# Residual rows of both routers turned back by TensorE, and the sparse attention's head in three rounded passes

## What is computed

```
for i in range(2):
    m = short_conv_mixer(x, ...) if i == 0 else dsa_mixer(x, ...)
    x = layer_norm(ALPHA * x + m, ln1_g[i], ln1_b[i])
    f = hier_moe(x, ...)        # router, then 64 experts of width 256, two for each token
    x = layer_norm(ALPHA * x + f, ln2_g[i], ln2_b[i])
```

## Time and profile before

| what | value |
|---|---|
| median of 3 runs | 2770.97 us (2769.46 to 2772.14) |
| the profiled execution | 2773.85 us, of which the span is 2772.0 us |
| busy share: PE, DVE, ACT, POOL | 90%, 49%, 29%, 4% |
| chain that ended last: PE, DMA, DVE | 64%, 23%, 7% |

### The profile page before, as it was taken

The page is one execution under the profiler, slowest core; times in us unless marked ns, Lnnn a source line. Parts: engine busy times, 40 slices in busy tenths (PEclk is TensorE's granted clock), DMA queues, the critical chain, the costliest instruction groups (busy, mean ns, idle before and its releaser), DMA issues.

```text
span 2772.0 us, 37468 instructions
## 1 busy us (share of the span) xinstructions
PE 2491.0 (90%) x14707; PEld 1794.8 (65%) x14708; DVE 1363.5 (49%) x2406; ACT 817.0 (29%) x1400; POOL 98.6 (4%) x80
## 2 busy tenths in 40 slices
PE   6999999999999999999888888878999978888887
PEld 4888788787678888787644444445765854444443
DVE  4555645633442225544654444434956474444444
ACT  3222333246232224322212112122367322121121
POOL 0000002000000000000020000003000030000000
PEclk9999999999999999999999999999999989999999
DMA  7655432401233332223389999984230449999976
GB/s 263 199 184 188 166 99 72 137 31 61 107 106 99 99 98 87 88 92 122 137 350 422 422 422 422 422 339 162 67 107 1 152 190 379 422 422 422 422 308 283
DMA packets 200620, 593.78 MB, mean 214 GB/s; under 512 B 9473, under 2 KB 125393, under 8 KB 151121
## 3 DMA queue, kind: packets, MB, share of 16 engines
q1 hardware_dynamic: 196736, 575.47, 54.0%
q0 software_dynamic: 3504, 16.63, 1.9%
...
HBM read 590.32 MB, written 7.41 MB: 216 GB/s over the span
## 4 chain that ended last, share of the span: by engine, by line
PE 64%; DMA 23%; DVE 7%; issue 3%; ACT 2%; SPq 1%; DVEq 0%; ACTq 0%
PE bank L1988 39%; DMA arena<-in_exp_w 17%; PE bank L2344 6%; PE bank L2078 5%; DMA ring<-in_exp_w 3%; PE bank L2364 2%; PE bank L2571 1%; SPq L579 1%; PE bank L2249 1%; PE bank L2468 1%; PE bank L2538 1%; PE bank L2168 1%; DVE ring_low L1207 1%; PE bank L2313 1%; PE bank L2371 1%
## 5 line engine op out<-in xcount | busy, mean ns | idle before, releaser
L1988 PE MATMUL bank<-parts 128*128 128x512 f32 x2624 | 817.8, 393 | 13.5 <-DVE parts L1446 5.5
L1988 PEld LDWEIGHTS bank<-parts 128*128 128x128 f32 x2624 | 493.5, 189 | 116.0 <-issue 7.5
L1988 PE MATMUL bank<-parts,ring_low 128*128 128x512 f32 x1312 | 513.7, 392 | 0.0
L1207 DVE TENSOR_TENSOR ring_low<-ring,parts 128x2048 fp32r<-128x2048 f32 x106 | 238.2, 2251 | 219.2 <-ACT parts L769 219.0
L2344 PE MATMUL bank<-ring,arena 128*32 128x256 f32 x2112 | 276.9, 417 | 54.2 <-DMA arena<-in_exp_w 54.2
L2344 PE MATMUL bank<-arena 128*32 128x256 f32 x2112 | 277.2, 417 | 28.9 <-issue 25.2
L769 ACT ACTIVATE parts<-ring 128x2048 fp32r<-128x2048 f32 x106 | 198.9, 1877 | 282.4 <-DMA ring<-in_w_ffn_in 123.1
L1988 PEld LDWEIGHTS bank<-parts,ring_low 128*128 128x128 f32 x1312 | 247.9, 189 | 52.1
L2371 PE MATMUL bank<-parts 128*128 128x512 f32 x496 | 169.2, 447 | 43.8 <-DVE parts L1731 23.0
L2344 PEld LDWEIGHTS bank<-ring,arena 128*32 128x32 f32 x2112 | 133.9, 115 | 110.5 <-issue 77.6
L1988 PE MATMUL bank<-ring_low 128*128 128x512 f32 x576 | 195.1, 397 | 1.7 <-ACT arena L1008 1.7
...
## 6 DMA issues: line engine op xcount, KB each, us to landing
arena<-in_exp_w SPq DMA_DIRECT2D x192, 1024.0 KB, 17.7
ring<-in_exp_w SPq DMA_DIRECT2D x192, 1024.0 KB, 19.5
...
```

Of the source, the lines that this page charges most:

```text
L1207: TTn(ring_low[:, n, 0:nk * cols], ring[:, n, 0:nk * cols], buf.bitcast(F32), ALU.subtract)\
L1988: i = mm(o, a[:, cols[0], cols[1]], b, start=first_ and n == 0, stop=last_ and n == 2)
```

## The change

1. **Residual, both routers.** POOL's eight instructions on `HT` and its loads of two rows are gone. PE turns `U` (which holds the same activation with gain and bias in it) back tile by tile into PSUM, 32 transposes of 128 x 128, between the router's steps, and ACT copies the 4 tiles of 128 x 1024 into `HT`. PE waits for the first copy ahead of the last tile, for two of them ahead of the first `gather` and for all ahead of the first turn. POOL's loads for the last norm come after it, with a wait in the last norm.
2. **Plan.** DVE's `rows_high` is moved ahead of two of the plan's steps (L1704, L1705).
3. **Head.** `c_kv`, `k_idx` and `w_idx` become one product of 200 columns in the tail (full float32), loaded as two pieces into one slot. `q_idx` is made in three passes. ACT rounds `U` by token tile in the norm (`rounded_rows`), DVE takes the rests so too (`row_rests`), the two index tiles of weights are rounded into `WHQ`. The loads of `stream_b` change slots and all of its first four wait for the last turn's `up` alone, not for its `down`.
4. **POOL's other eight instructions** (L731, L736) wait for the choice of keys (`mask`), where they ran beside the head.

```diff
-for n, c in enumerate((8, 9, 10)):
-    stream_b.append((tall(A["attn_w_in"], 256 * c, 256 if c < 10 else 200), KT, 256 if c < 10 else 200,
-                     ("qi_mm", "qi_mm", "kv_mm")[n], (1, 3, 2)[n]))
+latent_index = [(tall(A["attn_w_in"], HEADS2 * LATENT, LATENT), 0, LATENT),
+                (tall(A["attn_w_in"], HEADS2 * LATENT + LATENT + IDX_HEADS * IDX_DIM, 72), LATENT, LATENT + 72)]
+stream_b.append((latent_index, KT, LATENT + 72, "kv_mm", TT))
+for n in range(2):
+    stream_b.append((tall(A["attn_w_in"], (HEADS2 + 1) * LATENT + 256 * n, 256), KT, 256, "qi_mm", 2 * n + 2))
...
             for n in range(len(stream_b)):
-                if n < 5:
-
-                    sp.wait_ge(sem("turn_y" if n < 2 else "turn_ab"), last * 2 + 2)
+                if n < 4:
+
+                    sp.wait_ge(sem("turn_ab"), last * 2 + 2)
                 else:
...
-        pool.wait_ge(sem("moe_logits"), 4 * layer + 4)
-        for v, row in enumerate((layer, 2 + layer) + ((5, 7) if layer else ())):
-            pool.dma_start(ROWS[:, v], lnrows[row].partition_broadcast(P)).then_inc(sem("ln_vectors"), 16)
-        pool.wait_ge(sem("xt_low"), 4 * layer + 4)
-        pool.wait_ge(sem("moe_plan"), layer + 1)
-        pool.wait_ge(sem("ln_vectors"), 160 if layer else 64)
-        for t in range(TT):
-            st.did(pool.tensor_tensor(HT[:, t], HT[:, t], ROWS[:, 0], ALU.mult))
-        for t in range(TT):
-            if t == 0:
-                st.wait()
-            pool.tensor_tensor(HT[:, t], HT[:, t], ROWS[:, 1], ALU.add).then_inc(sem("resid"), 1)
-        if layer == 0:
+        if layer:
+            pool.wait_ge(sem("resid_tp"), 8)
+            for v, row in ((2, 5), (3, 7)):
+                pool.dma_start(ROWS[:, v], lnrows[row].partition_broadcast(P)).then_inc(sem("ln_vectors"), 16)
+        else:
...
-            pool.wait_ge(sem("ln_vectors"), 80)
+            pool.wait_ge(sem("ln_vectors"), 48)
             pool.wait_ge(sem("lt"), 16)
+            pool.wait_ge(sem("mask"), 5)
             for t in range(TT):
...
             pool.dma_start(ROW2, lnrows[6].partition_broadcast(P)).then_inc(sem("ln_vectors"), 16)
-            pool.wait_ge(sem("ln_vectors"), 96)
+            pool.wait_ge(sem("ln_vectors"), 64)
             for t in range(TT):
...
+    def rounded_rows(t):
+        act.wait_ge(sem("u_high"), 4 + t + 1)
+        act.wait_ge(sem("u_low"), 4 + t + 1)
+        A_(UQ[0][:, :, P * t:P * t + P], U[:, :, P * t:P * t + P], ACT.Copy).then_inc(sem("t_high"), 1)
+
     def layer_norm(j):
...
                 rounded_tokens(j, t - 1)
+            if j == 1 and t >= 2:
+                rounded_rows(t - 2)
         if j < 3:
             lifted(j, 3)
+        if j == 1:
+            rounded_rows(2)
+            rounded_rows(3)
         if j in (0, 2):
...
                accum_out=RK[:, 68 + t:69 + t]).then_inc(sem("moe_ge"), 1)
+        def residual_back(t):
+
+            act.wait_ge(sem("xt_low"), 4 * l + t + 1)
+            act.wait_ge(sem("resid_tp"), 4 * l + t + 1)
+            for h in range(2):
+                x = A_(HT[:, t, 512 * h:512 * h + 512], bank[RESID_BANKS[t][h]][:], ACT.Copy)
+            x.then_inc(sem("resid"), 1)
+
+        residual_back(0)
+        residual_back(1)
         act.wait_ge(sem("moe_m"), 2 * l + 2)
         A_(RK[:, 76:80], RK[:, 72:76], ACT.Exp).then_inc(sem("moe_ge"), 1)
+        residual_back(2)
+        residual_back(3)
...
+    weights_high(split_at["dsa_qi"])
+    weights_high(split_at["dsa_qi"] + 1)
     weights_high(split_at["dsa_q"])
+    act.wait_ge(sem("var"), 1)
+    A_(DS[:, 216:224], DS[:, 192:200], ACT.Sqrt).then_inc(sem("sdev"), 1)
     for t in range(4):
...
         evac(QI[:, t], bank[t][:], "qi")
-    for k in range(KT):
-        tile_high(UQ[0][:, k], U[:, k])
-    weights_high(split_at["dsa_q"] + 1)
-    act.wait_ge(sem("var"), 1)
-    A_(DS[:, 216:224], DS[:, 192:200], ACT.Sqrt).then_inc(sem("sdev"), 1)
+        if t == 1:
+            weights_high(split_at["dsa_q"] + 1)
     def query(h):
...
         st.wait()
+        dve.wait_ge(sem("ln_vectors"), 32)
+        rows_high(i0)
         seq(TTn(past, past, turns.unsqueeze(1).broadcast_to([P, MAX_TURNS, QUADS]), ALU.mult))
         seq(nc.vector.tensor_reduce(before_it, past, AXX, ALU.add))
-        dve.wait_ge(sem("ln_vectors"), 32)
-        rows_high(i0)
         st.did(TSc(LANDS[:, of_layer], at_quad, 16.0, 16.0 + 16 * QUADS * l, ALU.mult, ALU.add))
...
+    def row_rests(t):
+        dve.wait_ge(sem("kv_mm"), t + 1)
+        dve.wait_ge(sem("t_high"), tiles_at["dsa_q"] + t + 1)
+        C = slice(P * t, P * t + P)
+        TTn(UQ[1][:, :, C], U[:, :, C], UQ[0][:, :, C].bitcast(F32), ALU.subtract).then_inc(sem("t_low"), 1)
+
+    row_rests(0)
+    row_rests(1)
+    weights_low(split_at["dsa_qi"])
     dve.wait_ge(sem("vb_mm"), 1)
...
     TSc(VB[0:HEADS2, 512:640], bank[5][0:HEADS2, 0:P], -1.0, None, ALU.mult).then_inc(sem("vb"), 1)
-
-    weights_low(split_at["dsa_q"])
-    dve.wait_ge(sem("kv_mm"), 1)
+    row_rests(2)
+    row_rests(3)
+    weights_low(split_at["dsa_qi"] + 1)
     sq = S2
     for t in range(TT):
-        src = bank[6][:, P * t:P * t + P]
-        st.did(nc.vector.tensor_copy(CKV[:, t], src))
+        at = 200 * (t % 2)
+        st.did(nc.vector.tensor_copy(CKV[:, t], bank[6 + t // 2][:, at:at + LATENT]))
     st.wait()
...
-    dve.wait_ge(sem("kv_mm"), 2)
     for t in range(TT):
-        st.did(nc.vector.tensor_copy(KI[:, t, 0:64], bank[7][:, 72 * t:72 * t + 64]))
-        st.did(TSc(W8[:, t], bank[7][:, 72 * t + 64:72 * t + 72], IDX_HEADS ** -0.5, None, ALU.mult))
+        at = 200 * (t % 2) + LATENT
+        st.did(nc.vector.tensor_copy(KI[:, t, 0:64], bank[6 + t // 2][:, at:at + 64]))
+        st.did(TSc(W8[:, t], bank[6 + t // 2][:, at + 64:at + 72], IDX_HEADS ** -0.5, None, ALU.mult))
     st.wait()
...
     nc.vector.tensor_copy(DS[:, 204:205], DS[:, 196:197]).then_inc(sem("var"), 1)
+    weights_low(split_at["dsa_q"])
     dve.wait_ge(sem("sdev"), 1)
...
     def moe(l):
+        def residual_back(t):
+            for h in range(2):
+                for k in range(4):
+                    x = tp(bank[RESID_BANKS[t][h]][:, P * k:P * k + P], U[:, 4 * h + k, P * t:P * t + P], ident)
+            x.then_inc(sem("resid_tp"), 1)
+
+        residual_back(0)
+        residual_back(1)
         pe.wait_ge(sem("moe_ge"), 7 * l + 2)
...
         x.then_inc(sem("moe_rank"), 1)
+        residual_back(2)
+        pe.wait_ge(sem("resid"), 8 * l + 1)
+        residual_back(3)
...
         i0 = first_turn(pe, l)
+        pe.wait_ge(sem("resid"), 8 * l + 2)
         gather(i0)
         rows(i0)
+        pe.wait_ge(sem("resid"), 8 * l + 4)
         landed = 16 * (QUADS * l + 1)
...
         pe.wait_ge(sem("u_high"), 4 + t + 1)
+        at = 200 * (t % 2)
         for k in range(KT):
-            x = mm(bank[6][:, P * t:P * t + P], U[:, k, P * t:P * t + P], chunk("b", 0)[:, k, 0:P],
+            x = mm(bank[6 + t // 2][:, at:at + 200], U[:, k, P * t:P * t + P], chunk("b", 0)[:, k],
                    start=(k == 0), stop=(k == KT - 1))
-        if t == TT - 1:
-            x.then_inc(sem("kv_mm"), 1)
+        x.then_inc(sem("kv_mm"), 1)
...
-    def qi(b, w, c0):
+    for t in range(TT):
+        pe.wait_ge(sem("t_high"), tiles_at["dsa_q"] + t + 1)
+    for c in range(2):
+        i = split_at["dsa_qi"] + c
+        w = both(i)
+        for n in range(2):
+            pe.wait_ge(*((sem("w_high"), i + 1), (sem("w_low"), i + 1))[n])
+            for j in range(2):
+                for k in range(KT):
+                    mm(bank[2 * c + j][:], w[n][:, k, P * j:P * j + P], UQ[0][:, k], start=(k == n == 0), stop=False)
+    for t in range(TT):
+        pe.wait_ge(sem("t_low"), tiles_at["dsa_q"] + t + 1)
+    for b in range(4):
+        w = both(split_at["dsa_qi"] + b // 2)[0]
         for k in range(KT):
-            x = mm(bank[b][:], w[:, k, c0:c0 + P], U[:, k], start=(k == 0), stop=(k == KT - 1))
-        return x
-
-    w = chunk("b", 0)
-    qi(0, w, P).then_inc(sem("qi_mm"), 1)
-    landed(pe, "b", 1)
-    qi(1, chunk("b", 1), 0).then_inc(sem("qi_mm"), 1)
-    qi(2, chunk("b", 1), P).then_inc(sem("qi_mm"), 1)
-    landed(pe, "b", 2)
-    w = chunk("b", 2)
-    qi(3, w, 0).then_inc(sem("qi_mm"), 1)
-    for t in range(TT):
-        for k in range(KT):
-            x = mm(bank[7][:, 72 * t:72 * t + 72], U[:, k, P * t:P * t + P], w[:, k, P:200],
-                   start=(k == 0), stop=(k == KT - 1))
-    x.then_inc(sem("kv_mm"), 1)
+            x = mm(bank[b][:], w[:, k, P * (b % 2):P * (b % 2) + P], UQ[1][:, k], start=False, stop=(k == KT - 1))
+        x.then_inc(sem("qi_mm"), 1)
```

33 lines of the change are left out of this document (20 added, 13 removed).

## The result

The changed kernel takes **2736.5 us** (median of 4 runs, 2733.3 to 2739.7) beside 2771.6 for the kernel before on the same chip (4 runs, 2769.5 to 2774.2): a ratio of 0.9873, 95% interval 0.9859 to 0.9887. The forecast was 2734.4, within 2727 to 2749. On a second and a third occasion it took 2736.8 (beside 2771.5, ratio 0.9873, 0.9857 to 0.9890) and 2731.7 (beside 2769.4, ratio 0.9863, 0.9847 to 0.9880).

The account below looks back on a forecast made before the run. Expert-weight loads on DMA were taken to bound the expert layers, with a PE and DVE chain through the head. Gains of 8.2 + 7.6 + 20.8 + 0 = 36.6 us from 2770.97 gave 2734.4, range 2727 to 2749.

Parts of the forecast that it names:

- POOL holds the picks, without it 4.1 us, `down` 8.9 us sooner: Turn 0: without POOL beside them DVE's picks take 4.1 us instead of 16.7; `down` at 1399.7 instead of 1408.60.
- The gaps of DMA close: Expert weight loads after turn 0: both DMA gaps close, gaining 6.4 us in layer 0 and 5.8 in layer 1.
- The loads start 1.8 us sooner in each layer: Router to expert loads: PE without a pause gathers at 0.23 us, so loads start 1.8 us earlier; bounds 0 and 2.2.
- Part 2: Plan: DVE's row copy, ahead of two 0.96 us steps, starts at once; `up` at about 1383.0 instead of 1384.9.
- Cost of the transposes: Router: 32 PE transposes and ACT's 8 copies fit idle time and cost nothing; a late fourth tile would cost 1 us.
- The head, 20.8 us: From last token tile to index scores: they start at 1917.9 instead of 1938.72, 20.8 us sooner; bounds 15 and 23.
- 16 us of waiting gone: Head: its gain explained as 27.66 + 7.11 turned into 22.5, 16 us of waiting gone, less the tail.
- Part 4, 0 us: Attention: POOL's 8 instructions overlap it by about 13 us but don't hold DVE's PSUM work; 0, other bound 13 us.
- wrong if the attention takes longer than 104 us: Attention beside POOL: a sign that would refute the forecast, the attention taking longer than 104 us.
- The sum: Whole kernel: 8.2 + 7.6 for the expert layers, 20.8 for the head, 0 for attention, 36.6 us gained.
- Rival A: A DMA gap half closes, the gather stays slow (1.8 us each) or the head loses 4 to 6; chance 0.22.
- Rivals B, C, D and E: B: POOL holds DVE in attention, 0.10; C: more gain, 0.06; D: nothing moves, 0.02; E: slower, extra turns, 0.04.

Follow-up runs that it names:

- no_pool: Kernel before without POOL's eight residual instructions in either router, nothing put in their place; executed once, layer 0 read: 451.2 us from first load to last `down`.
- lag: Changed kernel with unneeded DVE comparisons ahead of turn 0's picks, 4 in layer 0 and 12 in layer 1; 2740.0 us beside 2731.7 for the changed kernel.
- plan_order: Changed kernel with the copy of the rows' high half put back behind the two plan steps; 2741.3 us beside 2736.8 for the changed kernel.
- after_again: The changed kernel measured and profiled once more, nothing altered; 2736.8 us.
- pool_head: Changed kernel without POOL's wait for the choice of keys, so its second eight residual instructions run in the head; 2743.8 us beside 2736.8.

## Why the prediction was right, point by point

- **POOL holds the picks, without it 4.1 us, `down` 8.9 us sooner:** right, 8.96; `no_pool` shows it to be the cause.
- **The gaps of DMA close:** right. The sizes, 6.4 and 5.8, were short by 0.8 and 1.2 in the first profile (by -0.4 to 1.2 in layer 1 over the three). The step read the loss off one window of 20 us at 68%; the distance between the first loads of two quads, less the 29.9 us that twelve loads fill, gives 7.3 and 7.0, and `lag` fits that form.
- **The loads start 1.8 us sooner in each layer:** wrong in layer 0 (30.7 to 30.95 instead of 30.83 in three profiles), and 0.9 to 2.2 us in layer 1. The failing step is the "and so" in the sentence that PE "now works from 1368 nearly to the gather, and so should make it at 0.23 us". The first half came true: 1368 is 9.9 us after the logits, and PE was busy from there (1370.8) to 0.75 us ahead of the gather. But the clock had fallen at 1369.0, in the pause of 4.35 us ahead of that work, which the prediction left out, and 6.6 us of work did not bring it back before the gather; the transposes and products ran at the lower level too. In layer 0 the step's bound of 0 was what came.
- **Part 2:** right as a mechanism, but it pays only behind a fast gather (one pair of profiles, layer 1 of `plan_order` and of `after_again`).
- **Cost of the transposes:** 0, right.
- **The head, 20.8 us:** measured 20.75, 20.0 and 20.8. Its terms hold as well: `qi` starts 34.6 us after the last `down` (34.1 forecast), takes 22.2 (22.5), the first queries 11.3 (11.2). One sentence of the sum is wrong beside that: "16 us of waiting gone". PE spent 7.55 of these 16 us on the high passes (L2493) and waited for 8.8; 34.8 - 22.5 + 16 - 3 would be 25 us, not 20.8. The forecast was right because it followed the engines' times and not this sentence. And 3.8 us of the gain is the low passes' clock, which the prediction has in its 11.2 us without naming it.
- **Part 4, 0 us:** right, 109.26 against 109.45 us for the attention, L1915 at 0.29 us. The sign "wrong if the attention takes longer than 104 us" doesn't say between which points; from the queries' end to the last products (L2571, now L2619) it was 104.2 before and is 104.0. That PSUM operands don't conflict was the trace's one row at 1389.18 and the Trainium skill's rule (SBUF — State Buffer, "SBUF: two separate sides"); `pool_head` shows the other half of the rule, for two SBUF operands: 12.39 instead of 4.54 us on L1879.
- **The sum:** 36.6 forecast, 37.0 measured behind the logits. 0.9 of that lies in the index scores, the queries and the attention, for which nothing was forecast. It came out so near by luck, because errors cancelled: 3.6 us forecast for the starts of the loads, of which 1.2 came in the first profile, against 1.9 too little for the gaps and those 0.9. Rival A's "the gather stays slow" was true by itself and cost 2.4 of its 3.6 us. Rivals B, C, D and E didn't occur; both layers have as many `down` products as before, so the same number of turns.
